# Grouping the two heads' triangular-inverse products in TensorE's instruction order

## What is computed

```
def rwkv_inputs(z, w0, w_up, a0, a_up, k_k, k_a):
    k = z[..., OFF_K:OFF_V]
    v = to_heads(z[..., OFF_V:OFF_WF])
    kk = to_heads(k * k_k)
    kk = kk * lax.rsqrt(jnp.maximum(jnp.sum(kk * kk, -1, keepdims=True), 1e-24))
...
def wkv_scan(S0, decay, k, v, kk, kka, r, reverse):
    def step(S, inp):
        w_t, k_t, v_t, kk_t, kka_t = inp[:5]
        sa = jnp.einsum('bhvk,bhk->bhv', S, kk_t)
        S = (S * w_t[:, :, None, :] - sa[..., None] * kka_t[:, :, None, :]
             + v_t[..., None] * k_t[:, :, None, :])
        y = jnp.einsum('bhvk,bhk->bhv', S, inp[5]) if want_y else None
        return S, y
```

## Time and profile before

| | |
|---|---|
| runs | 4062.73, 4067.24, 4070.47 us |
| the profiled execution | 4079.55 us, of which the span of instructions is 4077.7 us |
| TensorE matmul busy in the span | 3880.4 us (95%), 51352 records |
| VectorE / ScalarE / GpSimd busy | 1687.0 (41%) / 1146.1 (28%) / 551.5 (14%) us |
| granted TensorE clock | 0.986 of full |

### The profile page before, as it was taken

One profiled execution on the slowest core, in us unless ns is written; L12 is line 12 of the kernel. 1 busy time (PEld: TensorE's weight loads), 2 busy tenths in 40 slices (PEclk: granted clock), 3 DMA queues, 4 the chain that ended last, 5 costly groups with the idle time before them and its releaser, 6 DMA issues.

```text
span 4077.7 us, 111806 instructions
## 1 busy us (share of the span) xinstructions
PE 3880.4 (95%) x51352; PEld 2546.8 (62%) x51352; DVE 1687.0 (41%) x2721; ACT 1146.1 (28%) x2003; POOL 551.5 (14%) x436
## 2 busy tenths in 40 slices
PE   7899999999999999999999988999998999999998
PEld 3566666666555555655555556666666556678887
DVE  2555566664862111322231254555555422122232
ACT  3444444442122000200000344444444221021001
POOL 0000000000032221122232000000000023213443
PEclk8999999999999999999999999999999999999999
DMA  5000000000333223211112300000010253242224
GB/s 205 25 9 24 25 25 25 25 22 28 108 131 104 93 88 95 79 61 62 52 62 73 123 25 9 23 23 23 23 34 21 68 194 114 83 144 92 85 89 129
DMA packets 76337, 277.40 MB, mean 68 GB/s; under 512 B 8672, under 2 KB 13024, under 8 KB 75488
## 3 DMA queue, kind: packets, MB, share of 16 engines
q1 hardware_dynamic: 67968, 235.96, 18.1%
q10 hardware_dynamic: 6624, 29.04, 1.9%
q0 software_dynamic: 1280, 5.24, 0.3%
HBM read 256.58 MB, written 13.63 MB: 66 GB/s over the span
## 4 chain that ended last, share of the span: by engine, by line
PE 90%; ACT 4%; issue 3%; DVE 2%; DMA 1%; POOL 0%; ACTq 0%; DVEq 0%; SPq 0%; POOLq 0%
PE psum L1156 17%; PE psum L1670 16%; PE psum L1040 12%; PE psum L741 11%; PE psum L1467 9%; PE psum L1602 6%; PE psum L1052 5%; PE psum L1562 3%; PE psum L1625 2%; PE psum L1188 2%; PE psum L732 2%; PE psum L1000 2%; DMA ring<-w_stream_in 1%; PE psum L1018 1%; PE psum L921 1%
## 5 line engine op out<-in xcount | busy, mean ns | idle before, releaser
L1156 PEld LDWEIGHTS psum<-arena 32*32 32x32 f32 (+3 forms) x40512 | 697.6, 117 | 375.4 <-issue 301.4
L1156 PE MATMUL psum<-arena 32*32 32x32 f32 (+4 forms) x40512 | 790.8, 208 | 105.4 <-issue 73.7
L1040 PE MATMUL psum<-arena,ring 128*128 128x512 f32 (+1 forms) x1408 | 573.1, 523 | 2.5 <-ACT arena L1858 1.6
L741 PE MATMUL psum<-arena,ring 128*128 128x512 f32 (+1 forms) x1264 | 463.1, 524 | 3.8 <-DVE arena L2552 3.8
L741 PEld LDWEIGHTS psum<-arena,ring 128*128 128x128 f32 x1264 | 238.8, 191 | 230.3 <-issue 200.7
L1670 PE MATMUL psum<-arena 128*128 128x384 f32 (+1 forms) x1344 | 368.6, 433 | 0.0
L1040 PEld LDWEIGHTS psum<-arena,ring 128*128 128x128 f32 x1408 | 239.2, 191 | 142.0 <-issue 115.5
L1670 PEld LDWEIGHTS psum<-arena 128*128 128x128 f32 x1344 | 255.4, 190 | 106.4
L2991 POOL DMA_DIRECT2D ya_spill<-arena x16 | 8.8, 550 | 1995.2 <-DVE arena L2552 1995.2
L1670 PE MATMUL psum<-arena,ring 128*128 128x384 f32 (+1 forms) x1008 | 278.5, 433 | 0.0
L1670 PEld LDWEIGHTS psum<-arena,ring 128*128 128x128 f32 x1008 | 191.6, 190 | 79.5
(11 more groups left out here) (175 smaller groups left out, 4428.6 us busy)
## 6 DMA issues: line engine op xcount, KB each, us to landing
ring<-w_stream_in SPq DMA_DIRECT2D x440, 512.0 KB, 3.8
x_spill<-arena ACTq DMA_DIRECT2D x2, 3072.0 KB, 8.7
arena<-x_spill ACTq DMA_DIRECT2D x16, 384.0 KB, 6.5
arena<-ya_spill ACTq DMA_DIRECT2D x6, 768.0 KB, 6.0
ring<-w_stream_in ACTq DMA_DIRECT2D x8, 512.0 KB, 6.4
arena<-x_in ACTq DMA_DIRECT2D x1, 3072.0 KB, 14.3
arena<-ups_in SPq DMA_DIRECT2D x16, 192.0 KB, 2.4
ya_spill<-arena POOLq DMA_DIRECT2D x8, 384.0 KB, 6.3
```

Source lines behind the costliest of these rows:

```text
L741: mm = eng.matmul(psum[0:lhs[k].shape[-1], tile, a - off:b - off], lhsT=lhs[k], rhs=rhs[k][:, a:b], start=(k == 0), stop=(k == len(lhs) - ...
L1040: mm = pe.matmul(bank(j, z=b - a), lhsT=w[k], rhs=hs[k][:, a:b], start=(k == 0), stop=(k == KT - 1))
L1156: return pe.matmul(out, lhsT=lhs, rhs=rhs, start=start, stop=stop, skip_group_check=True)
```

## The change

Only strings of TensorE's order are changed: those of turn 1 and of turns 2 to 7, in both layers. In each of the four strings letters s are moved next to one another. Turn 8 and all lists of VectorE and ScalarE stay as they are. Two of the four changed lines (the other two are those of turn 1):

```
 WEAVE.update((("PE", 0, t), (
-    "xxdsxsdssdxxssxdxxdddxsddsdddsxddddsddxdsddddsddsddsdsddsxddsdddsddsdddsdddsddddsddsdxddsdddsdsdssss"
+    "xxdsxsdssdxxssxdxxdddxssdddddssxddddddxdssddddddssdddssddxddssdddddssddddddssddddddsdxddsdddsdsdssss"
     "sddssdsssdsssddsdssdssssssssssssssssssssssdsssssss")) for t in range(2, KT))
...
 WEAVE.update((("PE", 1, t), (
-    "xxsssdsxssxxdxxddddsxdsdxsddddsdddsdddsdddxsdsddsddsddsddsddsxdsddsxdsdsddxsddddsddsdsssddssdsssssds"
+    "xxsssdsxssxxdxxddddssxddxssdddddddssddddddxssdddssddddssddddssxdddssxddsddxsddddsddsdsssddssdsssssds"
     "ssdssssdddsssssssssssssssssssssssssss")) for t in range(2, KT))
```

More of the change, by code:

```diff
@@ L168 @@
 WEAVE.update((("PE", 0, t), (
-    "xxddxdxxdxsdssddddssxxsxdxdddxddxdddsdxdsdsdddsdddsssddsdddsdddsddsdsddsddddssddsdsddsdddssdssddddss"
+    "xxddxdxxdxsdssddddssxxsxdxdddxddxdddssdxddssddddddssssdddddssdddddssdddssddddssdddsddsdddssdssddddss"
     "ddsdssssssssssssssssssssssssssssssssssssssss")) for t in (1,))
 WEAVE.update((("PE", 0, t), (
-    "xxdsxsdssdxxssxdxxdddxsddsdddsxddddsddxdsddddsddsddsdsddsxddsdddsddsdddsdddsddddsddsdxddsdddsdsdssss"
+    "xxdsxsdssdxxssxdxxdddxssdddddssxddddddxdssddddddssdddssddxddssdddddssddddddssddddddsdxddsdddsdsdssss"
     "sddssdsssdsssddsdssdssssssssssssssssssssssdsssssss")) for t in range(2, KT))
@@ L186 @@
 WEAVE.update((("PE", 1, t), (
-    "ddddxsdxxssxsddxdssxdxxdddddddssdddsxdxsdsxdddddssdddsddsdssdsdssdsddxddsdsxddddsddssssssddsdssssssd"
+    "ddddxsdxxssxsddxdssxdxxdddddddssdddssxdxdssxdddddssdddddssdssddssdssddxdddsxddddsddssssssddsdssssssd"
     "sssssssdssssssssssssssssssssssssss")) for t in (1,))
 WEAVE.update((("PE", 1, t), (
-    "xxsssdsxssxxdxxddddsxdsdxsddddsdddsdddsdddxsdsddsddsddsddsddsxdsddsxdsdsddxsddddsddsdsssddssdsssssds"
+    "xxsssdsxssxxdxxddddssxddxssdddddddssddddddxssdddssddddssddddssxdddssxddsddxsddddsddsdsssddssdsssssds"
     "ssdssssdddsssssssssssssssssssssssssss")) for t in range(2, KT))
```

## The result

The changed kernel takes 4221.8 us (median of 4 runs, 4212.8 to 4247.2); the kernel before took 4067.7 beside it (4 runs, 4062.7 to 4070.5). The ratio is 1.039, with a 95% interval of 1.034 to 1.044: 154 us slower. The forecast was 4132, with a range up to 4180. The direction was right and the size was not.

The account below looks back on a forecast made before the run. TensorE's own list was taken to bound the kernel, busy 3880.4 of 4077.7 us. Fewer shape changes (-28), new waits (+49) and instruction holes (+44) gave +65 on the 4067.2 median: 4132 us, range 4082 to 4180.

Parts of the forecast that it names:

- Term 1: TensorE's list: 168 fewer changes of tile shape, 84 round trips at 0.33 us each, gain -28 us.
- Terms 2 and 3: TensorE's new waits for data not made sooner, +49 us; holes between 256-instruction blocks at 109 product pairs, +44 us.
- The three places of layer 0: New TensorE waits per turn at T1 and U1 of head 1 and R0k0: 0.8, 1.4 and 0.85 us.
- the three places of layer 0 for which no rows were taken: Waits at la2, kkn0 and T4 of head 1, taken at 0.85 us each, 2.55 us a turn.
- U4 of head 1: Layer 1: TensorE waits 0.5 us for this product's mask in each of six turns.
- the upper ends: Waits of 60 and holes of 109 us give +141, 4208 us; chance 0.05.
- the fetch keeps up with the list: Rival: TensorE's instruction holes add nothing; gain and waits alone give +21, 4088 us; chance 0.08.
- the gain is all that is left: Rival: TensorE's waits and holes together stay under 28 us; -28 us, 4039 us; chance 0.07.
- (1): Sign: 32x32 products show as rows of up to 192 records, 0.82 us longer than 96 where no hole.
- (2): Sign: TensorE's waits name L2617, L2601, L1858 and L1869, mostly in layer 0, 1 to 1.5 us before U1 of head 1.
- (3): Sign: "issue" idle before L1156 grows by tens of microseconds, in holes up to 2 to 2.8 us, 256 instructions apart.
- (4): Sign: layer 0's scan phase grows more than layer 1's.

Follow-up runs that it names:

- t_only: Kernel before, with only the first product of each level (T) having its two heads back to back, the second (U) as before: ratio 1.0136.
- half_after: Changed kernel issuing every second matmul of a product, two chunks wide, so it computes another result: ratio 0.9744.
- masks_first: Changed kernel with VectorE's order putting both heads' masks of a level together, and both subtractions and turns; TensorE's order kept: ratio 1.0380.
- the half kernels: Kernel before and changed kernel, each issuing every second matmul of a product, two chunks wide: ratios 0.9672 and 0.9744.
- select: Kernel before with only T3, T4 and U1 of layer 1 and U3 of layer 0 paired in turns 2 to 7: ratio 1.0054.
- pad_before_224: Kernel before with 224 already met waits at the start of TensorE's list: ratio 0.9973; its profiled execution took 12518 us.

## Why the prediction was wrong, point by point

**The step that failed** is the sum, -28 + 49 + 44: it has no term for TensorE's clock. The prediction found waits and holes of 0.5 to 2.8 us, priced each at its own length, and never asked what TensorE does behind a stop. All gaps of 1 us and more (from one record's start to the next one's, begun at the full clock) in the scan phases of the kernel before, the changed one, t_only to half_after (ten traces), by their length, and in how many of them the clock fell in the gap or within 2.5 us of its end:

```
gap, us        gaps   followed by a fall
1.0 to 1.4      379       50   13%
1.4 to 1.8      154       55   36%
1.8 to 2.2       91       63   69%
2.2 and more    141      114   81%
```

Counted by idle time alone the stops are fewer and the order is the same: 17%, 56%, 80% and 82%. Taken from the other side, 241 of the 244 falls in these phases came in such a gap or within 2.5 us of one, and those stretches make up 15% of the time at the full clock. The kernel before has 11 gaps of 1.8 us or more and the changed one 41. A projection between two products covers part of a hole or a wait; the pair leaves it as one stop. What the lower clock costs is worked out from the table of runs: busy time, in ten kernels against before, follows 0.41 us for each microsecond at the lower clock and 0.112 us for each change of shape (a fit; the ten residuals are up to 4.3 us). 0.41 x (218.4 - 58.0) = **+66 us**. TensorE is busy for 93% of those stretches in the changed kernel, so one half would have made 0.47; the rest of the difference isn't explained.

**Term 1, -28.** The mechanism is right and the size too large. The fit gives 168 x 0.112 = **-19 us**. half_after has the same 168 fewer changes with hardly a fall of the clock: busy time 8.2 us less, and 0.41 x 20.4 = 8.4 us of lower clock in it, so about -17. A round trip costs 0.2 us here, not 0.33. The 0.20 on the projection's side would be enough. I added 0.13 on the product's side; that it is the overlapping end of the last record is likely, not shown.

**Terms 2 and 3, +49 and +44.** Together they forecast 93 us of idle time, and it rose by **81.5**. Split by the releaser, waits for VectorE and ScalarE rose from 34.4 to 67.5 us, +33 where 49 were forecast; "issue" rose from 76.3 to 125.7, +49 where 44 were. The three places of layer 0 came out nearly as worked out, in each of the six turns: 0.65 us at T1 of head 1 (0.8 forecast), 1.22 at U1 of head 1 (1.4) and 0.78 at R0k0 (0.85). What was too large is the price of the three places of layer 0 for which no rows were taken: 2.55 us a turn forecast, 1.2 measured (L1869 and L1807, 7.1 us in all). In layer 1 the new wait for L1869 is 0.87 us in five turns (0.85 forecast for la3) and V0k0 waits 0.5 (0.5), but U4 of head 1 waits only in two turns, 0.30 us. The waits were also added to the holes as if they were independent, and masks_first shows that one takes the place of the other; here that cost the forecast little, since the holes alone came out above their 44.

**The sum as measured:** -19 + 81.5 + 66 = +128.5, against 131.8 in the traces. With the clock's term the forecast's own figures would have been -28 + 93 + 66 = +131, 4198 us. The medians are 154 us apart, since the profiled execution of the changed kernel was its fastest and that of the kernel before lay 12 us above its median.

**The range** was missed for the same reason: 4180 was the top of the waits and holes as worked out, and the upper ends (chance 0.05) were waits and holes again. No rival had a clock in it. A sign was there: the kernel before already has 58 us at the lower clock, and 7 of its 11 gaps of 1.8 us and more were followed by falls.

**The rivals.** That the fetch keeps up with the list is refuted: every long "issue" hole lies at a block boundary, and the half kernels have hardly any. The Trainium skill, "Runtime: NRT & Kernel Launch", section "Instruction fetch mechanics", says that a boundary between blocks of 256 instructions is mostly hidden. By number that holds here, since 76 of 342 boundaries in the phases before and 80 after show a hole over 0.3 us; by time it doesn't, since they cost 76 us before and 126 after. That the gain is all that is left needs waits and holes under 28 us; they are 81.5.

**What would show it.** (1) Rows of up to 192 records: yes, 1.84 us at 2836.88. (2) The waits name L2617, L2601, L1858 and L1869: yes. (3) "issue" in front of L1156 grows: yes, in holes of up to 2.6 us in layer 0 and 3.1 in layer 1 (3.1 before too), at block boundaries. (4) Layer 0 grows more: 75.9 against 55.9 us, yes. All four were right in the main, and none could tell 4132 from 4222: none looked at the granted clock. **What stays open:** why U's pairs meet more long stops than T's (103 against 51 us), why select spent 20 us more at the lower clock than the kernel before, and what the met waits in front of the list did in pad_before_224, which has no trace of an ordinary execution.

## What to carry to other kernels

Where an engine's idle time is going to grow, ask how it will be cut up, not only how much of it there is: here gaps of 1.0 to 1.4 us were followed by a fall of the clock in 13% of the cases, gaps of over 1.8 us in 76% (177 of 232), at 0.4 us for each microsecond spent at the lower level. The small matmuls of these products use up instructions faster than they arrive; about a microsecond of other work between two groups of them costs 0.2 us in changes of shape, and saved some 100 us over 109 pairs, 0.9 us each, with its changes of shape paid. Put the granted clock of a stretch into the list of things that would prove a forecast wrong.

## What was unexpected of the hardware

- TensorE's granted clock dropped to 1.2 GHz for 3.4 to 13.7 us behind stops of 1 to 3 us, in an execution whose mean clock is still 0.967. On the page this is a digit of 8 instead of 9 in a few slices; in the phases it is 160 us more at the lower level.
- A wait that is removed can come back in full as a hole in the instruction stream (13.1 us of waits less 8.7, holes 8.3 more, and no time won).
- 96 or 224 waits that are already met, put in front of TensorE's list, made the kernel before 0.2 to 0.3% faster. Two of them share one instruction.
- Every hole over 0.3 us without a semaphore, 839 of 840 in thirteen kernels, lies within three instructions of one place in a block of 256.
- Half the instructions for the same columns took 134 us off the kernel, though a 32x64 record takes 216 ns where a 32x32 one takes 194: the number of instructions weighed more in these products than their columns.
